# Spreading the decay rows with one bf16 product of three parts, and transposing v one step later

## The chip, the cores and the metric

The kernel runs on one core of a Trainium2 chip. The metric is the device time of one execution in microseconds (us); less is better. The engines of the core are TensorE (PE; its weight loads are listed as PEld), VectorE (DVE), ScalarE (ACT), GpSimd (POOL), SyncE (SP, which here only issues transfers) and the DMA engines.

## What is computed

Two layers of a decoder trunk over 256 tokens of width 1024. Layer 0 mixes by attention, layer 1 by a gated DeltaNet; after each mixer comes a mixture of experts (32 experts, top 2). All numbers are float32. The change lies in the DeltaNet, of which this much matters:

```python
h = x @ w_in                                    # qkv, z, b, a
qkv = silu(causal_dwconv(qkv, conv_w))          # 4 taps
q, k = l2norm(q), l2norm(k)                     # 8 heads of 128; v: 16 heads of 128
beta = sigmoid(b)
g = -exp(a_log) * softplus(a + dt_bias)
gc = cumsum(g)                                  # the decays, one row of numbers per head
decay = where(lower, exp(gc[:, None] - gc[None, :]), 0)
l_mat = where(strict, (k * beta) @ k.T * decay, 0)
# (I + l_mat) is inverted; u, w, the state and the output follow from it
o = o * rsqrt(mean(o * o) + eps) * norm_g * silu(z)
```

## The kernel before, in words

The order of work on every engine is written out by hand; engines meet only at counting semaphores.

**The projection steps.** The q, k and v channels are projected in 16 steps n = 0 to 15 of two 128-channel blocks each (q and k in steps 0 to 7, v in steps 8 to 15). In a step PE does `project(n, 0)` and `project(n, 1)` (L901, 8 products of 128 x 256 each), ACT copies the result out and scales it by one tap (`taps`), DVE adds the three other taps (`conv`, six instructions, L1700), ACT takes the tanh (L1265), and DVE makes the silu of it (L1690). Each engine runs through the same n in a loop of its own, so step n on DVE waits for step n on PE through ACT.

**The decay rows.** In steps 6 to 9 PE also calls `decay_rows` and `products` before each of the two projections, for the head pairs hk = 0 to 7. For each of the two heads of a pair, `decay_rows` needs the head's row of summed decays on all 128 partitions of a PSUM bank, 384 numbers wide (three blocks of 128). It gets it with a float32 product of a one-hot column, broadcast, and the 16 rows `g_row` (L928), and adds the causal mask with a bf16 product (L930). Then ACT takes the exponential of the bank (L1244 and L1245, four instructions a pair, semaphore `dt_sb`), and DVE multiplies it into the k k products (`decayed`, L1716). `decay_rows(hk)` waits for the exponentials of hk - 1, since both write banks 6 and 7. `g_row` is copied by ACT out of PSUM in step 3.

**The inversion.** From step 10 on DVE also inverts the 32 x 32 diagonal blocks: `blocks_in` (four transposes, L1730), then 31 calls of `eliminate` (L1738, L1740), five in each of the steps 11 to 15 and six behind them.

**The transposes of v.** `v_tokens(m)`, m = 8 to 15 (L957, four transposes on PE), waits for silu m (semaphore `si_sb`). It stands behind projection m + 2, the last two elsewhere. Its result is copied out by ACT (`evacuate_v`). vT has two buffers, so silu m on DVE, for m of 10 and more, waits until `v_tokens(m - 2)` is done (semaphore `vt_ps`).

**The z blocks.** Behind the steps PE does `z_block(0)` to `z_block(3)` (L971, eight products of 128 x 512), each followed by two `products(1, .)` (L944, L945). ACT takes a tanh of each block (`gate_z`, L1258); DVE then does, for each block, `z_gated` (L1722), two `decayed(1, .)` and one transpose of the inverse. Before the first `z_gated` it waits for all eight `v_tokens`:

```python
                dve.wait_ge(init, 8)
                dve.wait_ge(vt_ps, GH)
                for i in range(2):
                    z_gated(i)
                    for e in range(2):
                        decayed(1, 2 * i + e)
                    inverse_out(2 * i, 0)
```

`products(1, hk)` waits for `la_sb` of 8 + hk - 1, that is for `decayed(1, hk - 2)`, whose PSUM bank it writes again. Behind the z blocks come the levels of the inversion, the solves, the output projection and the experts of layer 1, each released by the work before it.

**The weights.** SP issues all loads of weights in one queue, each behind a count of PE's semaphores: the DeltaNet loads 3 to 10 behind `cv_ps` (projections done), the later ones behind `z_ps` (z blocks done). GpSimd sets one tile to zero (L583) behind `vt_ps` of 8.

Of the kernel before, what the change touches and what calls it, by code (L numbers as in the profile page):

```python
# [15 lines left out]
BF16 = mybir.dt.bfloat16  # L16
# [3 lines left out]
ALU = mybir.AluOpType  # L20
# [24 lines left out]
BLK = 32  # L45
INV = VH * NT
GROUPS = VH // 4
SOLVE_BANKS = (2, 3, 6, 7)
O_BANKS = ((4, 5), (6, 7), (0, 1), (2, 3))
EARLY = 5  # L50
# [139 lines left out]
def build(nc, a, out):  # L190
    with ExitStack() as ctx:
        def sb(name, shape, dt=F32):
            return ctx.enter_context(nc.sbuf_tensor(name, shape, dt))
# [18 lines left out]
        eps = sb("eps", [P, 1])  # L212
        mask_bf = sb("mask_bf", [P, P], BF16)
        ident_bf = sb("ident_bf", [P, 3, P], BF16)
        psum = [ctx.enter_context(nc.psum_tensor(f"bank{i}", [P, HALF], F32)) for i in range(8)]

        def k(name):
            at, w = COLS[name]
            return const[:, at:at + w]
# [71 lines left out]
        r = area(16, [VH, NT, GD])  # L291
        go = r
        ba_T = area(28, [SEQ])
        g_row = area(30, [3, P])
        xc = area(32, [2, 2, TAPS - 1 + SEQ])
        cv = area(36.0625, [2, 2, SEQ])
        ce = area(40.0625, [2, 2, SEQ])
# [294 lines left out]
        def _(pe):  # L592
# [266 lines left out]
            def gdn():  # L859
# [58 lines left out]
                def decay_rows(hk):  # L918

                    if hk == 0:  # L920
                        pe.wait_ge(gr_sb, 2)
                        pe.wait_ge(cw_sb, 1)
                    else:
                        pe.wait_ge(dt_sb, 4 * hk)
                    for e in range(2):
                        h = 2 * hk + e
                        bank = psum[6 + e][:, 0:384]
                        mm(bank, ident[0:VH, h:h + 1].to_broadcast([VH, P]),  # L928
                           g_row[0:VH].rearrange("p x c -> p (x c)"), start=True, stop=False)
                        last = mm(bank, mask_bf[:], ident_bf[:].rearrange("p x c -> p (x c)"), start=False, stop=True)  # L930
                    last.then_inc(row_ps, 1)

# [43 lines left out]
                for n in range(16):  # L976
                    for i in range(2):
                        if 6 <= n < 10:
                            decay_rows(2 * (n - 6) + i)
                            products(0, 2 * (n - 6) + i)  # L980
                        project(n, i)
                    if n == 0:
                        gate_tokens()
                    if n == 2:
                        decay_sums()
                    if 2 <= n < 10:
                        squares(n - 2)
                    if n >= 10:
                        v_tokens(n - 2)
                v_tokens(14)  # L990
                for i in range(4):
                    if i == 1:
                        v_tokens(15)
                    z_block(i)
                    for e in range(2):
                        products(1, 2 * i + e)

# [127 lines left out]
        def _(act):  # L1125
# [3 lines left out]
            def copy(o, i, **kw):  # L1129
                return do(o, i, ACT.Copy, **kw)  # L1130
# [86 lines left out]
            def gdn():  # L1217
# [37 lines left out]
                def gate_z(i):  # L1255

                    act.wait_ge(z_ps, i + 1)
                    do(zt[:, i], psum[i % 2][:], ACT.Tanh, scale=0.5).then_inc(zt_sb, 1)  # L1258

                for n in range(17):  # L1260
                    if n >= 1:
                        act.wait_ge(cv_sb, 2 * n)
                        if n >= 3:
                            act.wait_ge(si_sb, n - 2)
                        do(ce[:, (n - 1) % 2], cv[:, (n - 1) % 2], ACT.Tanh, scale=0.5).then_inc(ce_sb, 1)  # L1265
                    if n == 1:
                        act.wait_ge(min_sb, 1)
                        act.wait_ge(gdn_in, 80)
                        do(a_log, a_log, ACT.Exp).then_inc(sp_sb, 1)
                        own.link(do(ba_ln, ba_ln, ACT.Exp))  # L1270
                        do(ba_ln, ba_ln, ACT.Ln, bias=1.0).then_inc(sp_sb, 1)
                    if n == 6:
                        act.wait_ge(ss_ps, 4)
                        do(ln_k.rearrange("p t h -> p (t h)"), psum[2][:, 0:NT * GH], ACT.Ln, bias=eps[:]).then_inc(lnk_sb, 1)
                        act.wait_ge(lnk_sb, 1)
                        own.link(do(norm_k, ln_k, ACT.Exp, scale=0.5))
                        act.wait_ge(col_sb, 1)
                    if 6 <= n < 10:
                        for e in range(2):
                            decays(2 * (n - 6) + e)  # L1280
                    if n < 16:
                        taps(n)
                    if n == 3:
                        act.wait_ge(gr_ps, 1)
                        row = psum[4][0:VH, 0:SEQ].rearrange("p (x c) -> p x c", x=2)
                        copy(g_row[0:VH, 0:2], row).then_inc(gr_sb, 1)
                        copy(g_row[0:VH, 2], row[:, 1]).then_inc(gr_sb, 1)
                    if 1 <= n <= 8:
                        m = n - 1
                        act.wait_ge(si_sb, m + 1)  # L1290
                        if m >= 2:
                            act.wait_ge(ss_ps, m - 1)
                        do(sq[:, m % 2], gq[:, m // 4, 2 * (m % 4):2 * (m % 4) + 2], ACT.Square).then_inc(sq_sb, 1)
                    if n >= 10:
                        evacuate_v(n - 10)
                act.wait_ge(si_sb, 16)
                gate_z(0)
                evacuate_v(7)
                for i in range(1, 4):
                    gate_z(i)  # L1300

                def part(q, n=1):
                    return slice(q * BLK, (q + n) * BLK)
# [69 lines left out]
        def _(dve):  # L1373
# [71 lines left out]
            def attention():  # L1445
# [24 lines left out]
                for s in range(TURNS):  # L1470
                    n = head_at(s)
                    if n is not None:
                        b = n % 4
                        dve.wait_ge(s_ps, n + 1)
                        if n >= 4:
                            dve.wait_ge(pT_ps, n - 3)

                        v.scalar_tensor_tensor(out=s_sb[:, b], in0=psum[n % 2][:, 0:384], scalar=-ATT_SCALE,
                                               in1=k("mask_a" if n < 8 else "mask_b"), op0=ALU.mult,
                                               op1=ALU.subtract).then_inc(s_read, 1)  # L1480
                        dve.wait_ge(s_read, n + 1)
                        own(v.tensor_reduce(out=neg_max[:, b, 0:1], in_=s_sb[:, b, 0:P], axis=AX, op=ALU.min))
                        own.link(v.tensor_reduce(out=neg_max[:, b, 1:2], in_=s_sb[:, b, P:384], axis=AX, op=ALU.min))
                        dve.sem_inc(max_sb, 1)
                    m = head_at(s - 2)
                    if m is not None:
                        b = m % 4
                        dve.wait_ge(exp_sb, 2 * m + 2)
                        own.link(v.reciprocal(row_sum[:, b], row_sum[:, b]))
                        own(v.tensor_scalar(out=s_sb[:, b, 0:P], in0=s_sb[:, b, 0:P], scalar1=row_sum[:, b, 0:1],  # L1490
                                            scalar2=None, op0=ALU.mult))
                        own.link(v.tensor_scalar(out=s_sb[:, b, P:384], in0=s_sb[:, b, P:384], scalar1=row_sum[:, b, 1:2],
                                                 scalar2=None, op0=ALU.mult))
                        dve.sem_inc(p_sb, 1)
                    if s in (2, 4, 6, 8):
                        rotate(4 + (s - 2) // 2)
                    if s == 10:
                        own(v.tensor_copy(upper_b[:], k("upper")))
                        own(v.tensor_copy(ones_b[:], k("ones")))
                        own(v.tensor_copy(mask_bf[:], k("mask_a")[:, 0:P]))  # L1500
                        own(v.tensor_copy(ident_bf[:, 0], ident))
                        own(v.memset(ident_bf[:, 1], 0.0))
                        own(v.tensor_copy(ident_bf[:, 2], ident))
                layer_norm(0)

            def route(layer):
# [148 lines left out]
            def gdn():  # L1655
# [96 lines left out]
                for n in range(16):  # L1752
                    if n >= 1:
                        silu(n - 1)
                    if n == 1:
                        gate_logs()
                    if n == 4:
                        dve.wait_ge(gr_ps, 1)
                        v.tensor_tensor(out=col_bias, in0=ln_beta, in1=psum[5][:, 64:96].rearrange("p (t h) -> p t h", t=NT),
                                        op=ALU.subtract).then_inc(gc_sb, 1)  # L1760
# [115 lines left out]
```

## Time and profile before

| | |
|---|---|
| time of the runs, us | 1430.59, 1430.96, 1434.89 (median 1430.96) |
| profiled execution, us | 1432.51 |
| its span in the trace, us | 1430.6 |
| busy in the span | PE 1161.7 us, DVE 399.6 us, ACT 224.4 us |
| mean granted TensorE clock | 0.945 of full speed |
| DeltaNet projection steps and z blocks | 640 to 850 us of the span |

The span is the time from the first to the last instruction of the profiled execution; its time has 1.9 us more around it. Times in the rows below are counted from the start of the span. In rows of a timeline, an idle time in brackets is that of the engine just before the row, with what ended it.

### The profile page before, as it was taken

To read this page: it belongs to the slowest core of one execution; us is meant where nothing else is said; L and a number is where in the kernel's file an instruction comes from. 1 tells how busy PE (TensorE), PEld (TensorE's weight loads), DVE (VectorE), ACT (ScalarE), POOL (GpSimd) and SP (SyncE) were. 2 spreads that over 40 slices of the span, in tenths; PEclk is the share of its full clock that TensorE was granted. 3 is DMA by queue.
4 is the path that set the end of the run, shared out by engine and by line. 5 is a ranking of instruction groups with operands and counts; after the bars stand their busy time and mean duration, and the time that the engine had idled before them with its cause. 6 is when DMAs were issued, how large, how long until landed. Compare 5 with 4: busy or idle time off the path is not lost. (4 is left out here: it accounts for less than half of the span.)

```text
span 1430.6 us, 34064 instructions
## 1 busy us (share of the span) xinstructions
PE 1161.7 (81%) x14947; PEld 732.3 (51%) x14947; DVE 399.6 (28%) x1126; ACT 224.4 (16%) x589; POOL 14.4 (1%) x28
## 2 busy tenths in 40 slices
PE   8898779877777776759999899988987776777774
PEld 4444355544444444438778458445554444445442
DVE  1344512211111111133348744143211111111113
ACT  0123111100000010114433114110110010000001
POOL 0000100000000000010000000000000000000000
PEclk9999899989999999989999999998999999999998
DMA  9631599999999999973133341749999999999995
GB/s 361 253 118 59 211 412 425 429 423 429 424 427 427 426 427 424 427 302 118 59 118 118 118 146 62 281 198 379 424 429 425 425 426 426 427 426 428 425 424 209
DMA packets 63139, 461.20 MB, mean 322 GB/s; under 512 B 3824, under 2 KB 4000, under 8 KB 30320
## 3 DMA queue, kind: packets, MB, share of 16 engines
q1 hardware_dynamic: 61680, 455.92, 77.7%
q0 software_dynamic: 1408, 4.56, 0.8%
q8 instruction: 38, 0.62, 0.2%
q14 instruction: 13, 0.11, 0.0%
HBM read 459.41 MB, written 1.05 MB: 322 GB/s over the span
## 5 line engine op out<-in xcount | busy, mean ns | idle before, releaser
L803 PE MATMUL bank<-ring,arena 128*32 128x128 f32 x5568 | 191.4, 292 | 121.7 <-DMA ring<-in_moe_w 101.5
L803 PEld LDWEIGHTS bank<-ring,arena 128*32 128x32 f32 x5568 | 167.2, 114 | 142.7 <-DMA ring<-in_moe_w 82.5
L803 PE MATMUL bank<-arena 128*32 128x128 f32 x2624 | 103.2, 318 | 74.7 <-DMA arena<-in_moe_w 66.1
L1130 ACT ACTIVATE arena<-bank 128x256 f32<-128x256 f32 (+5 forms) x200 | 84.8, 431 | 368.6 <-PE bank L766 145.2
L1624 DVE SCALAR_TENSOR_TENSOR gated<-gated,bank 128x128 f32<-128x128 f32 x64 | 18.5, 288 | 428.4 <-ACT gated L1204 428.4
L763 PE MATMUL bank<-x,arena 128*32 128x256 f32 x1024 | 130.0, 637 | 4.5 <-DVEq L1585 4.5
L803 PEld LDWEIGHTS bank<-arena 128*32 128x32 f32 x2624 | 88.6, 125 | 85.8 <-DMA arena<-in_moe_w 79.3
L901 PE MATMUL bank<-xT,ring 128*128 128x256 f32 x512 | 115.2, 382 | 0.0
L901 PEld LDWEIGHTS bank<-xT,ring 128*128 128x128 f32 x512 | 96.6, 192 | 13.0 <-issue 0.4
L1204 ACT ACTIVATE gated<-bank 128x128 f32<-128x128 f32 x64 | 17.8, 278 | 466.7 <-PE bank L803 466.7
L784 PE MATMUL bank<-arena 32*128 32x256 f32 x1056 | 86.5, 444 | 4.8 <-issue 3.6
L639 PE MATMUL bank<-ring,xT 128*128 128x512 f32 x192 | 87.0, 606 | 2.3 <-DVEq L1466 2.0
L817 PE MATMUL bank<-ring,hT 128*32 128x256 f32 x1408 | 85.1, 382 | 3.3 <-DMA ring<-in_moe_w 3.3
L1630 DVE COPY arena<-bank 128x256 f32<-128x256 f32 x62 | 26.3, 425 | 185.0 <-PE bank L766 185.0
L784 PEld LDWEIGHTS bank<-arena 32*128 32x128 f32 x1056 | 54.2, 211 | 26.6 <-issue 21.4
L639 PEld LDWEIGHTS bank<-ring,xT 128*128 128x128 f32 x192 | 36.2, 194 | 44.6 <-issue 43.9
L971 PE MATMUL bank<-ring,xT 128*128 128x512 f32 x128 | 58.8, 613 | 0.0
L817 PEld LDWEIGHTS bank<-ring,hT 128*32 128x32 f32 x1408 | 41.6, 109 | 33.0 <-issue 10.7
L1100 PE MATMUL bank<-ring,arena 128*128 128x512 f32 x128 | 55.9, 594 | 1.6 <-ACT arena L1130 1.6
L763 PEld LDWEIGHTS bank<-x,arena 128*32 128x32 f32 x1024 | 29.4, 119 | 51.0 <-issue 38.9
L1633 DVE COPY arena<-bank 128x256 f32<-128x256 f32 x64 | 27.2, 425 | 99.1 <-PE bank L817 99.1
L1700 DVE SCALAR_TENSOR_TENSOR arena<-arena,cw 128x256 f32<-128x256 f32 x96 | 42.3, 482 | 40.2 <-ACT arena L1130 38.8
(229 smaller groups left out, 990.6 us busy)
## 6 DMA issues: line engine op xcount, KB each, us to landing
ring<-in_moe_w SPq DMA_DIRECT2D x131, 2048.0 KB, 40.5
arena<-in_moe_w SPq DMA_DIRECT2D x61, 2048.0 KB, 40.0
ring<-in_gdn_w_in SPq DMA_DIRECT2D x12, 2048.0 KB, 8.8
ring<-in_ab_w_in SPq DMA_DIRECT2D x5, 2048.0 KB, 23.1
ring<-in_gdn_w_out SPq DMA_DIRECT2D x4, 2048.0 KB, 8.6
ring<-in_ab_w_out SPq DMA_DIRECT2D x2, 2048.0 KB, 19.6
ring<-in_ab_w_in SPq DMA_DIRECT2D x2, 1024.0 KB, 8.2
x<-in_x SPq DMA_DIRECT2D x2, 512.0 KB, 4.4
```

The source lines that it names most:

```text
L639: last = mm(psum[4 + t][:], xT[:, j, t * P:(t + 1) * P], ring[:, slot_att(n), j], start=(j == 0), stop=(j == DJ - 1))
L763: mm(psum[4][h * CAP:(h + 1) * CAP, 0:Q].rearrange("p (c q) -> p c q", c=2), pick[:, b, t], by_j[:, h::TILES], start=(t == 0), stop=(t == ...
L784: last = mm(psum[h][:, t * Q:(t + 1) * Q], gpT[part, b, t], y_e[part], start=False, stop=stop and t == NT - 1, skip_group_check=not (stop ...
L803: last = mm(psum[5][h * CAP:(h + 1) * CAP, m * FH:(m + 1) * FH], xeT[:, j], slot_tile(slots[m])[:, j, h // 2 * SEQ + h % 2:(h // 2 + 1) * ...
L817: last = mm(psum[7][h * CAP:(h + 1) * CAP, 0:Q], hT[:, g], w2[:, g // 2, g % 2, h * Q:(h + 1) * Q], start=(g == 0), stop=(g == TILES - 1), ...
L901: last = mm(psum[n % 2][:, i * SEQ:(i + 1) * SEQ], ring[:, slot_gdn(n // 2), j, ch * P:(ch + 1) * P], xT[:, j], start=(j == 0), stop=(j == ...
L971: last = mm(psum[i % 2][:], xT[:, j, t * P:(t + 1) * P], ring[:, slot_gdn(8 + zz), j], start=(j == 0), stop=(j == DJ - 1))
L1100: last = mm(psum[GDN_OUT + 2 * h + t][:], goT[:, 8 * g + c, t * P:(t + 1) * P], ring[:, slot_gdn(12 + 2 * g + h), c], start=(g == 0 and c ...
L1130: return do(o, i, ACT.Copy, **kw)
L1630: o2.link(v.tensor_copy(gpT[:, (b + 1) % GROUP].rearrange("p t q -> p (t q)"), psum[5][:, 0:SEQ]))
L1633: o2.link(v.tensor_copy(y_e, psum[7][:, 0:Q]))
L1700: ins = v.scalar_tensor_tensor(out=cv[:, b, i], in0=xc[:, b, i, tap:tap + SEQ], scalar=cw[:, at:at + 1], in1=cv[:, b, i], op0=ALU.mult, op ...
```

## The change

Two edits.

1. The fp32 product of `decay_rows` becomes a bf16 one. The decay rows are split into three bf16 parts whose sum is the float32 value: the value rounded to bf16, the rest rounded to bf16, and the rest of that. They stand at partitions 0, 32 and 64 of `g_row`, which becomes a bf16 tile of 80 rows with zeros between, and the one-hot column `head_bf` (bf16) picks the head's row of all three parts, so that one product adds them. DVE sets the tile to zero in step 2 and makes the parts in step 3 (five instructions); ACT, which made two copies in step 3, makes one in step 4. `head_bf` is made by DVE in the attention of layer 0.
2. `v_tokens(m)` stands behind projection m + 3 in place of m + 2: those of 8 to 12 behind projections 11 to 15, that of 13 ahead of `z_block(0)`, that of 14 behind `z_block(0)`, that of 15 behind `z_block(1)`. Before, that of 14 stood ahead of `z_block(0)` and that of 15 ahead of `z_block(1)`. `evacuate_v` on ACT moves with them.

```diff
+G_ROWS = 2 * 32 + VH
...
+        head_bf = sb("head_bf", [P, VH], BF16)
...
-        g_row = area(30, [3, P])
+        g_rest = area(29, [SEQ])
+        g_mid = area(30, [SEQ], BF16, 2)
+        g_row = area(30.5, [3, P], BF16, 2)
...
                     if hk == 0:
-                        pe.wait_ge(gr_sb, 2)
+                        pe.wait_ge(gr_sb, 4)
...
-                        mm(bank, ident[0:VH, h:h + 1].to_broadcast([VH, P]),
-                           g_row[0:VH].rearrange("p x c -> p (x c)"), start=True, stop=False)
+                        mm(bank, head_bf[0:G_ROWS, h:h + 1].to_broadcast([G_ROWS, P]),
+                           g_row[0:G_ROWS].rearrange("p x c -> p (x c)"), start=True, stop=False)
...
-                    if n >= 10:
-                        v_tokens(n - 2)
-                v_tokens(14)
+                    if n >= 11:
+                        v_tokens(n - 3)
                 for i in range(4):
-                    if i == 1:
-                        v_tokens(15)
+                    if i == 0:
+                        v_tokens(13)
                     z_block(i)
+                    if i < 2:
+                        v_tokens(14 + i)
                     for e in range(2):
                         products(1, 2 * i + e)
...
-                    if n == 3:
-                        act.wait_ge(gr_ps, 1)
-                        row = psum[4][0:VH, 0:SEQ].rearrange("p (x c) -> p x c", x=2)
-                        copy(g_row[0:VH, 0:2], row).then_inc(gr_sb, 1)
-                        copy(g_row[0:VH, 2], row[:, 1]).then_inc(gr_sb, 1)
+                    if n == 4:
+                        act.wait_ge(gr_sb, 3)
+                        copy(g_row[0:G_ROWS, 2], g_row[0:G_ROWS, 1]).then_inc(gr_sb, 1)
...
-                    if n >= 10:
-                        evacuate_v(n - 10)
+                    if n >= 11:
+                        evacuate_v(n - 11)
                 act.wait_ge(si_sb, 16)
-                gate_z(0)
-                evacuate_v(7)
-                for i in range(1, 4):
+                for i in range(4):
                     gate_z(i)
+                    if i < 2:
+                        evacuate_v(6 + i)
...
+                        own(v.tensor_copy(head_bf[:], k("stack")[:, 0:VH]))
...
+                    if n == 2:
+                        own(v.memset(g_row[0:G_ROWS].rearrange("p x c -> p (x c)"), 0.0))
+                    if n == 3:
+                        dve.wait_ge(gr_ps, 1)
+                        own.wait()
+                        row = psum[4][0:VH, 0:SEQ]
+                        first, mid = (g_row[at:at + VH, 0:2].rearrange("p x c -> p (x c)") for at in (0, 32))
+                        last = g_row[64:64 + VH, 0:2].rearrange("p x c -> p (x c)")
+                        v.tensor_copy(first, row).then_inc(gr_sb, 1)
+                        dve.wait_ge(gr_sb, 1)
+                        own.link(v.tensor_tensor(out=g_rest[0:VH], in0=row, in1=first, op=ALU.subtract))
+                        own.link(v.tensor_copy(g_mid[0:VH], g_rest[0:VH]))
+                        v.tensor_copy(mid, g_mid[0:VH]).then_inc(gr_sb, 1)
+                        v.tensor_tensor(out=last, in0=g_rest[0:VH], in1=g_mid[0:VH], op=ALU.subtract).then_inc(gr_sb, 1)
```

## Rows read from the trace of the kernel before

**Rows 1.** Groups of the page, most costly first: expert products of layers 0 and 1.
```profile
L803 PE MATMUL bank<-ring,arena 128*32 128x128 f32 x5568 | 191.4, 292 | 121.7 <-DMA ring<-in_moe_w 101.5
```

**Rows 2.** Busy time of the engines, steps 10 to 15: stretch, its length, then each engine.
```profile
745.00:803.00 58.00, 53.14 (x241) 43.23 (x241) 50.57 (x114) 17.67 (x41) 0.12 (x1) 0.97 0.41 141
```

**Rows 3.** Timeline of PE, steps 6 to 8 (start us, us, engine, line, operation).
```profile
695.70 0.91 PE L928 MATMUL bank<-arena,const 16*128 16x384 f32 x2 [0.55 <-ACT ring L1245]
...
701.93 0.95 PE L914 MATMUL bank<-const,arena 128*128 128x1 f32 x8
702.81 0.91 PE L928 MATMUL bank<-arena,const 16*128 16x384 f32 x2
703.65 0.34 PE L930 MATMUL bank<-ident_bf,mask_bf 128*128 128x384 bf16 x1
703.91 0.91 PE L928 MATMUL bank<-arena,const 16*128 16x384 f32 x2
704.75 0.34 PE L930 MATMUL bank<-ident_bf,mask_bf 128*128 128x384 bf16 x1
704.92 0.59 PE L944 MATMUL bank<-arena 128*128 128x256 f32 x2
...
709.13 0.91 PE L928 MATMUL bank<-arena,const 16*128 16x384 f32 x2
...
715.35 0.95 PE L914 MATMUL bank<-const,arena 128*128 128x1 f32 x8
```

**Rows 4.** Timeline of ACT, step 7.
```profile
702.13 0.60 ACT L1130 ACTIVATE arena<-bank 128x512 f32<-128x512 f32 x1 [2.75 <-PE bank L901]
...
706.24 0.63 ACT L1265 ACTIVATE arena<-arena 128x512 f32<-128x512 f32 x1 [2.27 <-DVE arena L1700]
...
707.74 0.37 ACT L1245 ACTIVATE ring<-bank,gates 128x128 f32<-128x128 f32 x1
```

**Rows 5.** Timeline of DVE: steps 3, 10 and 12, then the first z block.
```profile
672.17 2.71 DVE L1700 SCALAR_TENSOR_TENSOR arena<-arena,cw 128x256 f32<-128x256 f32 x6 [5.15 <-ACT arena L1130]
...
747.94 7.88 DVE L1730 STREAM_TRANSPOSE y<-ring 32x1024 f32<-32x1024 f32 x4
...
766.27 0.69 DVE L1690 SCALAR_TENSOR_TENSOR arena<-arena 128x512 f32<-128x512 f32 x1 [0.76 <-issue]
...
802.63 0.19 DVE L1740 TENSOR_TENSOR y<-y,arena 128x31 f32<-128x31 f32 x1
803.03 0.69 DVE L1722 SCALAR_TENSOR_TENSOR arena<-arena,bank 128x512 f32<-128x512 f32 x1 [0.20 <-DVE y L1740]
803.63 1.81 DVE L1716 TENSOR_TENSOR ring<-bank,ring 128x768 f32<-128x768 f32 x2
```

**Rows 6.** Timeline of PE: behind projection 12, then from projection 15 to `z_block(2)`.
```profile
764.69 0.60 PE L957 MATMUL bank<-const,arena 128*128 128x128 f32 x4
...
786.73 0.60 PE L957 MATMUL bank<-const,arena 128*128 128x128 f32 x4
792.18 1.12 PE L957 MATMUL bank<-const,arena 128*128 128x128 f32 x4 [4.86 <-DVE arena L1690]
793.09 7.98 PE L971 MATMUL bank<-ring,xT 128*128 128x512 f32 x16
800.91 0.59 PE L944 MATMUL bank<-arena 128*128 128x256 f32 x2
...
802.22 0.60 PE L957 MATMUL bank<-const,arena 128*128 128x128 f32 x4
802.65 7.03 PE L971 MATMUL bank<-ring,xT 128*128 128x512 f32 x16
...
810.83 7.03 PE L971 MATMUL bank<-ring,xT 128*128 128x512 f32 x16
```

**Rows 7.** Stretches of 1 us; behind the engines, the granted clock (1.00 is full speed).
```profile
690.00:691.00 1.00, 1.00 (x5) 0.84 (x4) 0.48 (x2) 0.48 (x1) 0.00 (x0) 0.50 1.01 365
...
793.00:794.00 1.00, 1.00 (x4) 0.48 (x3) 0.93 (x3) 0.29 (x1) 0.00 (x0) 0.50 1.06 414
```

## Prediction

> **What bounds the kernel now.** I began with the groups of the page. Most of the time is in the experts, where PE waits for weights to arrive [rows 1]; the change does not touch that, but it decides what a gain in layer 1's mixer is worth. Every load there is issued behind a semaphore count of PE or DVE, none at a fixed time, so if the DeltaNet ends x us sooner, the experts of layer 1 start and end x us sooner. The question is by how much PE reaches the work behind the z blocks sooner.
>
> The timelines give the stretch around the change. In steps 6 to 9 PE runs without a gap: a step takes 715.35 - 701.93 = 13.42 us [rows 3], and DVE and ACT wait for it. From step 10 on the bound changes. DVE takes in the blocks for 7.88 us at 747.94 and then has no gap over 0.8 us until its last elimination ends at 802.82 [rows 5]; in 745 to 803 it is busy 50.57 of 58 us, the rest being mostly the short spaces between dependent instructions [rows 2]. PE is ahead of it, until `v_tokens(14)` has to wait 4.86 us for DVE's silu [rows 6]. So the stretch has two limits in a row: PE sets when DVE starts its long chain (step 9), and DVE sets when it ends. What shortens PE before step 10 moves DVE's whole chain; what shortens PE after that only helps as far as DVE lets it.
>
> **Edit 1, the rows.** For a head, L928 takes 703.65 - 702.81 = 0.84 us and L930 0.26 (703.65 to 703.91) or, for the second head, 0.17 (704.75 to 704.92): 2.11 us for a pair [rows 3]. The new product streams the same 384 columns in bf16, once, as L930 does. Its cost on the stream is not in the trace for 80 rows; the nearest rows bound it: 0.17 where the weight load is hidden, 0.26 where it isn't. Four such products make 0.68 to 1.04 us a pair. I take 0.80, nearer to the hidden end, because the 80 rows are nearer to the 128 of the products before which the load was hidden (L944) than to the 16 before which it wasn't (L928). A pair saves 1.31 us (1.07 to 1.43).
>
> By the Trainium skill (TensorE: Matmul & The Clock Gate, Back-to-back issue gap) a warm product of 384 columns takes 384/2.4 + 2.5 ns, about 0.16 us, so an estimate from that page for the pair is 0.65 us and the saving 1.46; the row of 0.17 agrees where the load is hidden, and the rule leaves out the 0.26.
>
> Does each saving reach the end of the step? The second `decay_rows` of a step waits for the exponentials of the first pair. Their chain starts where projection 1 of the step before ended: PE goes on to L914 at 701.93, ACT copies from 702.13, DVE convolves, the tanh starts at 706.24, and the last of the four exponentials ends at 707.74 + 0.37 = 708.11 [rows 4]. With a few hundredths for the semaphore the second L928 could start 6.22 us after 701.93. PE itself will be there after 0.88 (L914, 701.93 to 702.81) + 0.80 + 4.21 (products and projection 0: 704.92 to 709.13) [rows 3] = 5.89. So ACT's chain, hidden by 1 us before, is now last by 0.33 us, and a step takes 6.22 + 0.80 + 4.11 (715.35 - 709.13 = 6.22, less the pair's 2.11) = 11.13 us, 2.29 less than 13.42. That holds for steps 7, 8 and 9. In step 6 the wait is there already, 0.55 us for L1245 at 695.70 [rows 3], so the saving of its first pair only lengthens the wait (to 1.9 us), and that of the second, 1.31, is left. Sum: 1.31 + 3 x 2.29 = 8.2 us. With 1.04 a pair it is 1.07 + 3 x 2.05 = 7.2, with 0.68 it is 1.43 + 3 x 2.41 = 8.7.
>
> What it adds: in step 2 a memset and in step 3 five short instructions on DVE. The copies of 16 rows or of a few dozen numbers are some 0.2 to 0.3 us each, with their waits under 2 us together; DVE idles 5.15 us in step 3 [rows 5], and the first user is step 6. Without that cover it would cost its 2 us. ACT swaps two short copies in step 3 for one in step 4, ahead of a square: under 0.3 us, where its gaps are 2.75 and 2.27 us in a later step [rows 4]. `head_bf` is one DVE copy in the attention, at most 0.2 us, if on the path at all. I put all three at 0 (0 to 0.3).
>
> **Edit 2, the transposes.** All times here are those of before, from which the 8.2 is then taken off. Projection 15 with its transposes ended at 786.73 + 0.43 = 787.16 (0.43 is 802.65 - 802.22) [rows 6]. Now `v_tokens(13)` ends there, and its silu has long been done. `z_block(0)` starts at 787.16 and not at 793.09. The block itself took 7.82 us in place of 6.87 (810.83 - 802.65 = 8.18, less the products' 1.31): the clock was at half after the wait [rows 7]. So: `z_block(0)` to 794.03, `v_tokens(14)` to 794.46 (its silu ended near 792.1), two products to 795.77, `z_block(1)` to 802.64, `v_tokens(15)` to 803.07, two products. Without a new wait `z_block(2)` would start at 804.38, 6.45 us sooner than 810.83.
>
> But there is a new wait. `products(1, 2)` needs `decayed(1, 0)`, and DVE reaches it only after the last elimination (802.82), after all eight `v_tokens` (now the last of them ends at about 803.24, a little later than the eliminations) and after `z_gated(0)`. That gives `z_gated` at 803.4 (before: 803.03), `decayed(1, 0)` from 804.0 to 804.9 and `decayed(1, 1)` to 805.8, from the 0.60 and 0.90 of [rows 5]. `products(1, 2)` starts at 804.95, `products(1, 3)` at 805.85, `z_block(2)` at 806.5: 2.1 us of new waiting, and 4.3 us gained. Queued behind the waiting product on PE are the z blocks and everything after them, so these 2.1 us count in full. From there PE leads again: DVE's turn for a block (0.6 + 1.8 + 2.2) is shorter than PE's 8.18, so the 4.3 us stay.
>
> Three queues that the edit moves past. Silu m waits for `v_tokens(m - 2)`, now one step later. The tightest I find is silu 11 at 766.27 [rows 5]: it will need the transposes that now stand where those at 764.69 stand [rows 6], 0.43 earlier, so ending near 764.9: 1.4 us of slack. Cost 0; without the slack it would land on the saturated DVE at full price. ACT's copies of v have their turns one step later behind the same taps; their results are wanted by transposes two heads on. SP's counts are of projections and z blocks; each load is issued sooner by what its releaser gains, so its distance to its use stays, and nothing is lost there. GpSimd's memset behind `vt_ps` is wanted only a level later.
>
> **Sum.** 8.2 + 4.3 = 12.5 us. The profiled execution would take 1432.51 - 12.5 = 1420.0; it is 1.55 above the median of the runs, so against the median 1430.96 I predict 1418.5.
>
> **The rivals.**
> (a) *The clock falls in one of the new waits.* At 690 to 691 the clock was at half (1.2 GHz) while PE was busy throughout, behind a run of small products and decay rows [rows 7], and part of that was hidden before the wait of 0.55 us. Now step 6 has a wait of 1.9 us, or about 3.5 if the clock does not fall in front of it, and `products(1, 2)` one of 2.1. The wait of 4.86 was followed by a stretch at half whose price was 0.48 on the transposes (793.09 - 792.18, less 0.43) and 0.95 on the z block, 1.4 us. One such fall in the open: 1418.5 + 1.4 = 1419.9; two: 1421.3. Against it: the wait of 0.55 cost nothing, and both new waits are well under 4.86. Chance of one or two 0.30. The Trainium skill (TensorE: Matmul & The Clock Gate, HAM oscillation) warns of idle gaps between bursts of products, after which the clock is at its lower level; the trace agrees for the wait of 4.86, and by that rule one fall more is 1.4 us more.
> (b) *The loop through ACT and DVE eats more of edit 1.* It is already the last by 0.33 us; each further us in a step costs one in each of three steps. At 1 us more the time is 1421.5; if edit 1 gives nothing and only edit 2 works, 1426.7. For it: the chain has no slack left. Against: its pieces were timed in a trace where only its start waited for PE, and DVE's `decayed` of the pair does not stand in it. Chance 0.14.
> (c) *Given back later*, by weights that don't come sooner: 1430. No load in the stretch is released by time, and no load ended a wait of PE in the timeline rows that I read there. Chance 0.05.
> (d) *Slower.* Silu m waits for the later transposes. The slack is 1.4 us; DVE is the bound in steps 11 to 15, so each us of lateness beyond it is lost once per step, six times. To outweigh 12.5 us PE must be late by 1.4 + 12.5/6 = 3.5 us against DVE in every step; at 5 us late the time is 1418.5 + 6 x 3.6 = 1440.1. It takes a clock at half through these steps, whose projections would double from 7 us. Chance 0.03.
> (e) *More than forecast*, below 1416.4: the new products or ACT's chain shorter than in the rows: 0.06.
>
> **How the numbers follow.** The forecast has what is left, 0.42, with 7.2 to 8.7 for edit 1 and 4.3 for edit 2: 1418.0 to 1419.5, and a us of scatter on each side (two of the runs differ by 0.4, one is 4 higher). For 8 in 10 I add (a) and the near half of (b): 1416.4 to 1423.0. A measurement of this kernel can tell about 0.3%, 4.3 us, from no change. Faster by more than that (below 1426.7) are the forecast, (a), (e) and nearly all of (b): 0.91; within it (c) and the rest of (b): 0.06; slower 0.03.
>
> **What would show it.** (Lines as of the kernel before.) L928 as 16 products of 80 rows with starts 0.17 to 0.26 us before the next; steps 7 to 9 at 11.1 us (from 13.42) with a wait of 0.3 for L1245 and step 6 with a wait for L1245 of 1.9 us or more; DVE's L1730 at about 739.7; no wait of L957 for L1690; a wait of L944 for DVE's L1716 of about 1.9 us and then one of 0.3 behind `z_block(1)`; `z_block(2)` at 798.3. The prediction is wrong if L930 is followed by gaps, if L1690 on DVE waits for L957, or if the clock column shows 0.50 somewhere between 696 and 830.

## The result and the profile after

| | before | after |
|---|---|---|
| median of the runs, us | 1435.49 (1430.59 to 1439.01, 6 runs) | 1422.49 (1419.77 to 1424.08, 6 runs) |
| profiled execution, us | 1432.51 | 1424.08 |
| its span, us | 1430.6 | 1422.2 |

The ratio of the runs is 0.9923, with a 95% interval of 0.9903 to 0.9942: 11 us faster (8 to 14). Forecast were 1418.5 in a range of 1416.4 to 1423.0, a ratio of 0.9913. The runs of before that came with the result were slower than the three shown ahead of it, so the ratio is the better measure of the two. For the profiled execution the forecast was 1420.0 us; it took 1424.08, 4.1 us more.

The timeline of PE after the change, with start, length, line and the idle time ahead; L932 is the new bf16 product, L934 the mask, L905 the projections, L918 the squares, L961 `v_tokens`, L948 `products`, L975 the z blocks. It answers to [rows 3] and [rows 6]:

```profile
689.12 0.95 PE L918 MATMUL bank<-const,arena 128*128 128x1 f32 x8
689.93 0.32 PE L932 MATMUL bank<-arena,head_bf 80*128 80x384 bf16 x1
690.10 0.33 PE L934 MATMUL bank<-ident_bf,mask_bf 128*128 128x384 bf16 x1
690.26 0.33 PE L932 MATMUL bank<-arena,head_bf 80*128 80x384 bf16 x1
690.42 0.33 PE L934 MATMUL bank<-ident_bf,mask_bf 128*128 128x384 bf16 x1
690.59 0.59 PE L948 MATMUL bank<-arena 128*128 128x256 f32 x2
...
698.62 0.34 PE L932 MATMUL bank<-arena,head_bf 80*128 80x384 bf16 x1 [3.76 <-ACT ring L1250]
...
700.77 4.46 PE L905 MATMUL bank<-xT,ring 128*128 128x256 f32 x16
705.07 0.95 PE L918 MATMUL bank<-const,arena 128*128 128x1 f32 x8
...
711.30 0.34 PE L932 MATMUL bank<-arena,head_bf 80*128 80x384 bf16 x1 [0.50 <-ACT ring L1250]
...
716.08 0.95 PE L918 MATMUL bank<-const,arena 128*128 128x1 f32 x8
...
738.10 0.95 PE L918 MATMUL bank<-const,arena 128*128 128x1 f32 x8
...
782.19 1.04 PE L961 MATMUL bank<-const,arena 128*128 128x128 f32 x8
783.07 7.03 PE L975 MATMUL bank<-ring,xT 128*128 128x512 f32 x16
...
798.55 0.60 PE L961 MATMUL bank<-const,arena 128*128 128x128 f32 x4
800.97 0.70 PE L948 MATMUL bank<-arena 128*128 128x256 f32 x2 [1.82 <-DVE ring L1720]
...
802.59 7.03 PE L975 MATMUL bank<-ring,xT 128*128 128x512 f32 x16
```

The reader is to see five things. A pair of decay rows takes 690.59 - 689.93 = 0.66 us. The steps 7, 8 and 9 take 716.08 - 705.07 = 11.01 us, with a wait of 0.50 for ACT in each. Step 6, from 689.12 to 705.07, takes 15.95 us, with a wait of 3.76. `v_tokens(12)` and `(13)` run together at 782.19 with no wait, and so does `v_tokens(14)`, which now stands behind `z_block(0)`: the wait of 4.86 us is gone. And PE has a new wait of 1.82 us, for DVE's `decayed(1, 0)`.

The granted clock of a stretch behind the wait of 3.76 us is the number behind the engines: 0.51, so the lower of the two levels (1.2 GHz), and the projection that starts in it takes 4.46 us in place of 3.62:

```profile
699.00:702.00 3.00, 3.00 (x10) 2.46 (x9) 1.43 (x2) 1.35 (x4) 0.00 (x0) 0.51 0.00 0
```

DVE and ACT, for [rows 4] and [rows 5]: the first and the last of the five new DVE instructions of step 3 with the `conv` behind them, the tanh and the last exponential of the first pair of step 7 on ACT, then DVE's long chain:

```profile
669.85 0.41 DVE L1769 CAST arena<-bank 16x256 bf16<-16x256 f32 x1
...
671.30 0.42 DVE L1774 TENSOR_TENSOR arena<-arena 16x256 bf16<-16x256 f32 x1
675.08 2.71 DVE L1704 SCALAR_TENSOR_TENSOR arena<-arena,cw 128x256 f32<-128x256 f32 x6 [3.37 <-ACT arena L1135]
```

```profile
709.38 0.63 ACT L1270 ACTIVATE arena<-arena 128x512 f32<-128x512 f32 x1 [2.27 <-DVE arena L1704]
...
710.87 0.38 ACT L1250 ACTIVATE ring<-bank,gates 128x128 f32<-128x128 f32 x1
```

```profile
743.84 7.85 DVE L1734 STREAM_TRANSPOSE y<-ring 32x1024 f32<-32x1024 f32 x4
...
762.14 0.69 DVE L1694 SCALAR_TENSOR_TENSOR arena<-arena 128x512 f32<-128x512 f32 x1 [0.76 <-issue]
...
798.88 0.19 DVE L1744 TENSOR_TENSOR y<-y,arena 128x31 f32<-128x31 f32 x1
```

DVE still idles 3.37 us behind its new instructions. The chain from the block transposes to the last elimination is as long as before, 799.07 - 743.84 = 55.2 us against 802.82 - 747.94 = 54.9, and silu 11 still has 0.76 us ahead of it and no wait for PE: the whole chain moved and kept its length to 0.3 us. (The 0.3 us stand ahead of silu 14, 1.12 us of idle time in place of 0.76. Edit 1 alone, where `v_tokens` stands as before, has them too, and edit 2 alone has not, so they are no wait for the later transposes.)

To compare kernels I use a stretch that leaves out what happens elsewhere: from the squares of step 5 (the first row above) to `z_block(2)`. Rows of PE of the kernel before that are not among those shown, the two groups ahead of the steps among them:

```profile
639.01 1.07 PE L869 MATMUL bank<-xT,wba 128*32 128x256 f32 x16 [0.87 <-DVE xT L1379]
640.01 7.17 PE L901 MATMUL bank<-xT,ring 128*128 128x256 f32 x32
...
686.21 0.95 PE L914 MATMUL bank<-const,arena 128*128 128x1 f32 x8
...
742.20 0.95 PE L914 MATMUL bank<-const,arena 128*128 128x1 f32 x8
```

and the same two of the kernel after:

```profile
639.61 1.93 PE L873 MATMUL bank<-xT,wba 128*32 128x256 f32 x16 [0.88 <-DVE xT L1382]
641.47 8.62 PE L905 MATMUL bank<-xT,ring 128*128 128x256 f32 x32
```

Before, the stretch takes 810.83 - 686.21 = 124.62 us; after, 802.59 - 689.12 = 113.47, so 11.15 less. From `z_block(2)` to the end of the span it is 619.8 before and 619.6 after: all that is won there stays. Ahead of the squares the profiled execution of after is 2.91 us later (0.60 at the gate columns, the rest in these two groups, which ran at the lower clock: 1.93 against 1.07 us and 8.62 against 7.17). In the kernel with edit 2 alone, where nothing of the change has run by then, the two groups took 1.94 and 7.92 us, and in the other experiments 1.93 or 1.94 and 7.85 to 8.38. So the one profile of before is the exception in having the gate columns at the higher clock, and nothing of the change is needed for the lower one. The three add up to the 8.4 us between the two profiled executions, and explain why these differ by less than the medians do.

### The profile page after: what moved, and what is told of

It is laid out like the page before. It is cut to its first block and busy times, and to the rows that moved or that the text cites. A ratio compares the mean times of both kernels' runs of the same rounds, so it can differ in the third digit from the quotient of the medians.

```text
span 1422.2 us, 34039 instructions
## 1 busy us (share of the span) xinstructions
PE 1149.7 (81%) x14931; PEld 726.4 (51%) x14931; DVE 401.2 (28%) x1133; ACT 223.8 (16%) x588; POOL 14.4 (1%) x28
## 5 line engine op out<-in xcount | busy, mean ns | idle before, releaser
L807 PE MATMUL bank<-ring,arena 128*32 128x128 f32 x5568 | 181.3, 282 | 119.5 <-DMA ring<-in_moe_w 97.1
L807 PEld LDWEIGHTS bank<-ring,arena 128*32 128x32 f32 x5568 | 159.4, 110 | 139.2 <-DMA ring<-in_moe_w 82.5
L807 PE MATMUL bank<-arena 128*32 128x128 f32 x2624 | 108.1, 329 | 81.5 <-DMA arena<-in_moe_w 77.4
L1135 ACT ACTIVATE arena<-bank 128x256 f32<-128x256 f32 (+4 forms) x198 | 84.1, 431 | 373.9 <-PE bank L770 147.1
L807 PEld LDWEIGHTS bank<-arena 128*32 128x32 f32 x2624 | 92.8, 129 | 92.4 <-DMA arena<-in_moe_w 86.7
L905 PE MATMUL bank<-xT,ring 128*128 128x256 f32 x512 | 116.3, 385 | 0.0
L905 PEld LDWEIGHTS bank<-xT,ring 128*128 128x128 f32 x512 | 97.6, 194 | 13.8 <-issue 0.8
L821 PE MATMUL bank<-ring,hT 128*32 128x256 f32 x1408 | 88.2, 392 | 3.3 <-DMA ring<-in_moe_w 3.3
L975 PE MATMUL bank<-ring,xT 128*128 128x512 f32 x128 | 58.4, 610 | 0.0
```

What stands on the lines that cost most here:

```text
L807: last = mm(psum[5][h * CAP:(h + 1) * CAP, m * FH:(m + 1) * FH], xeT[:, j], slot_tile(slots[m])[:, j, h // 2 * SEQ + h % 2:(h // 2 + 1) * ...
L821: last = mm(psum[7][h * CAP:(h + 1) * CAP, 0:Q], hT[:, g], w2[:, g // 2, g % 2, h * Q:(h + 1) * Q], start=(g == 0), stop=(g == TILES - 1), ...
L905: last = mm(psum[n % 2][:, i * SEQ:(i + 1) * SEQ], ring[:, slot_gdn(n // 2), j, ch * P:(ch + 1) * P], xT[:, j], start=(j == 0), stop=(j == ...
L975: last = mm(psum[i % 2][:], xT[:, j, t * P:(t + 1) * P], ring[:, slot_gdn(8 + zz), j], start=(j == 0), stop=(j == DJ - 1))
```

## The experiments

In each, "the stretch" is the one just defined; before 124.62, changed kernel 113.47. The line numbers shift by a few from kernel to kernel. Each kernel has one profile, and a ratio is always that of its timed runs to those of the kernel before.

**Edit 1 alone.** The v parts as in the kernel before:

```diff
-                    if n >= 11:
-                        v_tokens(n - 3)
+                    if n >= 10:
+                        v_tokens(n - 2)
+                v_tokens(14)
...
```

> Edit 1 alone; v_tokens and evacuate_v stand as before. My theory (PE sets when DVE's long chain starts, DVE sets when it ends): DVE's L1730 starts sooner by edit 1's whole saving, 7.0 us as in the changed kernel if the clock falls behind the wait of step 6 (8.6 if not), the wait of v_tokens(14) for silu 14 stays at 4.9 us and z_block(2) comes 7.0 us sooner than before, counted from the squares of step 5: 117.6 us between them (before 124.62, changed kernel 113.47). Time about 7 us under the kernel before. Rival (the two edits only work together, since PE waited 4.9 us for DVE anyway): the wait grows by 7 us and the time moves by under 2.

Measured: ratio to before 0.9954 (0.9939 to 0.9968). PE:

```profile
733.83 0.95 PE L918 MATMUL bank<-const,arena 128*128 128x1 f32 x8
784.15 1.11 PE L961 MATMUL bank<-const,arena 128*128 128x128 f32 x4 [5.19 <-DVE arena L1693]
785.06 9.39 PE L975 MATMUL bank<-ring,xT 128*128 128x512 f32 x16
```

The stretch, from 685.02 to 804.22, is 119.2 us: 5.4 less than before, 1.6 less than expected. From the squares of step 5 to those of step 9 it won 7.2 us (7.0 expected). The wait for silu 14 stayed (5.19 us, not 7 more), and the clock was at its lower level behind it for longer than in the kernel before: `z_block(0)` took 9.39 us and not 7.98, which is where the 1.6 went. So edit 1 moves DVE's chain, as forecast, and the rival falls.

**Edit 2 alone**, the fp32 product of before with the v parts of after.

> Edit 2 alone, with the fp32 product of before. My theory: from the squares of step 5 to z_block(2) 120.3 us (4.3 less than before), with a new wait of products(1, 2) for DVE's first decayed(1, 0) of about 1.9 us; time 4 us under before. Rival 1 (the wait only moves): under 1 us gained, the new wait about 5 us. Rival 2 (the whole wait and its stretch at half clock are won): 118.2 us, 6.4 less.

Measured: ratio 0.9957 (0.9936 to 0.9978).

```profile
687.43 0.95 PE L914 MATMUL bank<-const,arena 128*128 128x1 f32 x8
...
696.93 0.91 PE L928 MATMUL bank<-arena,const 16*128 16x384 f32 x2 [2.23 <-ACT ring L1246]
...
746.75 0.95 PE L914 MATMUL bank<-const,arena 128*128 128x1 f32 x8
...
809.62 0.70 PE L944 MATMUL bank<-arena 128*128 128x256 f32 x2 [1.82 <-DVE ring L1717]
811.25 7.03 PE L971 MATMUL bank<-ring,xT 128*128 128x512 f32 x16
```

From step 9's squares to `z_block(2)` it is 811.25 - 746.75 = 64.5 us against 810.83 - 742.20 = 68.6 before: 4.1 us won, with the same new wait of 1.82. The first part of the stretch, which the edit does not touch, was 3.3 us longer in this profile (59.3 against 56.0), with the clock at its lower level at 707 to 710 and at 735 to 737 while PE was busy; so the whole stretch was 123.8 us, 0.8 under before and not the expected 4.3. These falls are not in the profile of before, whose fall at 689 is not in this one: they come and go. And without that fall the wait of step 6 is 2.23 us and not 0.55, while the step takes 15.73 us against 15.72. The two edits alone won 6.6 and 6.2 us in the timed runs, together 11.0: within their intervals (4.6 to 8.7, 3.2 to 9.2, 8.3 to 13.9) they add, and so do the parts of the stretch that each moves, 7.2 + 4.1 = 11.3 against 11.15.

**One more step later.** Does lateness of the transposes cost as I said in rival (d)?

```diff
-                    if n >= 11:
-                        v_tokens(n - 3)
+                    if n >= 12:
+                        v_tokens(n - 4)
                 for i in range(4):
                     if i == 0:
+                        v_tokens(12)
                         v_tokens(13)
...
```

ACT's copies of v move one step back too, the sixth of them behind silu 15.

> The changed kernel with v_tokens one more step later: 8 to 11 behind projections 12 to 15, 12 and 13 ahead of z_block(0), 14 and 15 as in the changed kernel. Silu 10 then waits for transposes behind projection 12, some 5 us later than it ran. My forecast's rival (d) says that lateness on the saturated DVE is lost once per step, six times: up to 30 us slower than the changed kernel, 1450 us. The other theory: the first wait pushes DVE's chain back by some 5 us, and after that DVE, whose steps of 8 us are longer than PE's 7.34, no longer waits: about 5 us slower than the changed kernel, once.

Measured: 1.0016 of before (0.9999 to 1.0033), so all that the change won is lost, some 13 us; the stretch is 129.1 us, 15.6 more than the changed kernel's. First DVE, then PE:

```profile
758.89 0.69 DVE L1696 SCALAR_TENSOR_TENSOR arena<-arena 128x512 f32<-128x512 f32 x1 [6.00 <-PE bank L961]
...
766.23 0.69 DVE L1696 SCALAR_TENSOR_TENSOR arena<-arena 128x512 f32<-128x512 f32 x1 [1.17 <-PE bank L961]
...
774.75 0.69 DVE L1696 SCALAR_TENSOR_TENSOR arena<-arena 128x512 f32<-128x512 f32 x1 [1.29 <-PE bank L961]
```

```profile
785.30 0.69 PE L961 MATMUL bank<-const,arena 128*128 128x128 f32 x4 [2.30 <-ACT arena L1136]
793.91 1.09 PE L961 MATMUL bank<-const,arena 128*128 128x128 f32 x4 [7.91 <-ACT arena L1136]
794.79 9.32 PE L975 MATMUL bank<-ring,xT 128*128 128x512 f32 x16
```

On DVE the other theory was right: beyond the 0.76 us that silu always waits, it lost 5.2 us once and 0.4 and 0.5 after it, not 6 us six times. But both theories missed where the rest went. `v_tokens(12)` and `(13)` write banks that ACT has to have copied out two heads earlier, and ACT makes those copies behind the tanh that waits for DVE. So PE stood 10.2 us in front of `z_block(0)`, with work ready behind it in its queue, and the clock fell. Rival (d)'s price per step was wrong, and its bound of where the change would turn slower too: one step further is enough to lose everything, by another queue.

**Few rows or an fp32 neighbour?** Only the first bf16 part is kept (`G_ROWS = VH`), so the decays are rounded to bf16 here, and DVE makes one instruction of the five in step 3.

> The changed kernel with the first bf16 part of the decay rows alone, so a product of 16 rows and not of 80 (the decays are then only as exact as bf16). I sized the product at 0.80 us a pair because I took the 0.26 us behind L930 for a price of a weight load of few rows; measured were 0.66 with 80 rows. If few rows are the cause, a pair takes 0.8 to 1.0 here; if it was the fp32 product behind it, 0.66 again.

Measured, one run:

```profile
704.00 0.33 PE L932 MATMUL bank<-arena,head_bf 16*128 16x384 bf16 x1
704.27 0.34 PE L934 MATMUL bank<-ident_bf,mask_bf 128*128 128x384 bf16 x1
704.53 0.33 PE L932 MATMUL bank<-arena,head_bf 16*128 16x384 bf16 x1
704.80 0.34 PE L934 MATMUL bank<-ident_bf,mask_bf 128*128 128x384 bf16 x1
704.97 0.59 PE L948 MATMUL bank<-arena 128*128 128x256 f32 x2
```

Each start is 0.27 us behind the last, and a pair takes 704.97 - 704.00 = 0.97, though all is bf16. With 80 rows a start is 0.16 to 0.17 behind the last. So it is the few rows: next to a product of 128 rows, one of 16 costs 0.1 us more on either side of it, one of 80 nothing. The rows of the weight loads show the 0.1 us: with 80 rows the load for the mask's product starts at 705.88 and the product at 706.04, so it is hidden behind the product before; with 16 rows they start at 704.26 and 704.27, so it is not. The forecast's upper bound, 0.26 for each product, was real, for another shape.

**The wait of step 6, filled.** Eight more fp32 products where PE waits; the output does not use them.

```diff
                         project(n, i)
+                        if n == 6 and i == 0:
+                            for j in range(8):
+                                mm(psum[3][:, SEQ:2 * SEQ], xT[:, j, 0:P], xT[:, j], start=True, stop=True)
```

> The changed kernel with eight more fp32 products of 128 x 256 (3.5 us, into an unused half bank) behind projection (6, 0), where PE waits 3.76 us for the exponentials of the first pair; the output is unchanged. Theory A: the clock's fall behind that wait is the wait's doing; with the wait filled it is gone, step 6 takes 14.3 us and not 15.95, and from the squares of step 5 to z_block(2) are 111.8 us and not 113.47. Theory B: it has to do with the decay rows and squares around it, as in the kernel before, where it came with PE busy: step 6 stays at 15.9.

```profile
685.51 0.95 PE L918 MATMUL bank<-const,arena 128*128 128x1 f32 x8
...
695.01 0.34 PE L932 MATMUL bank<-arena,head_bf 80*128 80x384 bf16 x1 [0.31 <-ACT ring L1253]
...
699.78 0.95 PE L918 MATMUL bank<-const,arena 128*128 128x1 f32 x8
```

Step 6 takes 14.27 us, no row of steps 6 to 9 is at the lower clock, and the stretch is 112.0: theory A. The ratio to before was 0.9866 (0.9838 to 0.9894, four runs), some 8 us under the changed kernel's, where the stretch accounts for 1.5. The profiled execution is 5.0 us under that of the changed kernel, and 3.6 of these are won ahead of the squares of step 5, where both do the same work; so the rest is not shown to be the filled wait's doing. With four runs, two at 1419 and two at 1411 us, I leave it open.

**The logarithm earlier.** What sets the wait is the work of ACT ahead of the first exponentials.

```diff
-                    if n == 6:
-                        act.wait_ge(ss_ps, 4)
-                        do(ln_k.rearrange("p t h -> p (t h)"), psum[2][:, 0:NT * GH], ACT.Ln, bias=eps[:]).then_inc(lnk_sb, 1)
-                        act.wait_ge(lnk_sb, 1)
-                        own.link(do(norm_k, ln_k, ACT.Exp, scale=0.5))
                         act.wait_ge(col_sb, 1)
...
                         do(sq[:, m % 2], gq[:, m // 4, 2 * (m % 4):2 * (m % 4) + 2], ACT.Square).then_inc(sq_sb, 1)
+                    if n == 5:
+                        act.wait_ge(ss_ps, 4)
+                        do(ln_k.rearrange("p t h -> p (t h)"), psum[2][:, 0:NT * GH], ACT.Ln, bias=eps[:]).then_inc(lnk_sb, 1)
+                        act.wait_ge(lnk_sb, 1)
+                        own.link(do(norm_k, ln_k, ACT.Exp, scale=0.5))
```

and DVE's subtraction of it stands ahead of silu 5.

> The changed kernel with ACT's logarithm and exponential of the norms (and their two table loads, 3.1 us) one step earlier, in ACT's gap behind the square of step 5, and DVE's short instruction that needs them ahead of silu 5. If that work of ACT sets the wait of 3.76 us, the wait is about 1.2, step 6 is 2.6 us shorter, and 1.7 more if the clock then does not fall: 109.2 us from the squares of step 5 to z_block(2), against 113.47. Rival: tanh 5 now comes 0.9 us later, DVE's silu too, and under 1 us is won.

Measured: 0.9889 (0.9869 to 0.9908); the stretch, 688.05 to 797.46, is 109.4 us, step 6 11.89.

```profile
695.17 0.34 PE L932 MATMUL bank<-arena,head_bf 80*128 80x384 bf16 x1 [1.38 <-ACT ring L1250]
...
699.94 0.95 PE L918 MATMUL bank<-const,arena 128*128 128x1 f32 x8
```

The 4.1 us are there, as expected, and the clock stays up behind a wait of 1.38.

**DVE's order behind silu 15.**

```diff
                 silu(15)
+                for e in range(2):
+                    decayed(1, e)
                 for k_ in range(5 * EARLY + 2, BLK - 1):
                     eliminate(k_)
...
                     z_gated(i)
-                    for e in range(2):
-                        decayed(1, 2 * i + e)
+                    if i:
+                        for e in range(2):
+                            decayed(1, 2 * i + e)
```

> The changed kernel with decayed(1, 0) and (1, 1) on DVE right behind silu 15, ahead of the last four eliminations. If the order on DVE, not its sum of work, makes products(1, 2) wait, that wait (1.82 and 0.33 us) is gone, and z_block(2), which needs z_gated(0), comes 2.0 us sooner: 111.4 us from the squares of step 5. Rival: z_gated(0) comes later by the 1.8 us of the two decayed, and z_block(2) waits for it: nothing won.

Measured: 0.9904 (0.9886 to 0.9922); the stretch is 112.4 us.

```profile
797.50 7.10 PE L975 MATMUL bank<-ring,xT 128*128 128x512 f32 x16 [1.19 <-DVE arena L1726]
```

Between the two: the wait of `products(1, 2)` is gone, and a part of it is back as a wait of 1.19 us of `z_block(2)` for `z_gated(0)`, which now comes later. 1.1 us won of the 2.0.

**All three together**: the earlier logarithm (e6), DVE's order (e7), and the exponentials of the first pair ahead of the tanh in steps 7 to 9:

```diff
+                    if 7 <= n < 10:
+                        decays(2 * (n - 6))
                     if n >= 1:
                         act.wait_ge(cv_sb, 2 * n)
...
                     if 6 <= n < 10:
-                        for e in range(2):
+                        for e in range(n > 6, 2):
                             decays(2 * (n - 6) + e)
```

> e6 and e7 together, and in steps 7 to 9 the exponentials of the first pair ahead of the tanh on ACT, where ACT idles 2.26 us and they take 1.34; that takes away the 0.50 us for which PE waits in each of these steps. 4.3 + 2.0 + 1.5: 105.7 us from the squares of step 5 to z_block(2), and about 8 us less than the changed kernel, ratio to before 0.987. Rival: the tanh is late and DVE's chain with it, and the three steps stay at 11.0 us: 107.2.

```profile
700.80 0.95 PE L918 MATMUL bank<-const,arena 128*128 128x1 f32 x8
...
711.15 0.95 PE L918 MATMUL bank<-const,arena 128*128 128x1 f32 x8
...
795.03 7.11 PE L975 MATMUL bank<-ring,xT 128*128 128x512 f32 x16 [0.84 <-DVE arena L1729]
```

Steps 7 to 9 take 10.35 us each, without a wait, and the stretch is 795.03 - 688.91 = 106.1 us. Median 1413.85 us, ratio to before 0.9860 (0.9840 to 0.9880, four runs): faster than both kernels.

## Which step of the prediction failed, and what was right

**The step that failed is step 6.** The forecast let the saving of its first pair go into the wait ("to 1.9 us") and kept that of the second, 1.31 us. The wait became 3.76, the clock fell behind it, and the step took 15.95 us against 15.72 (701.93 - 686.21) before: 0.2 lost in place of 1.31 won. The forecast had read the wait of 0.55 as the step's own, though in that profile PE reached it late, at the lower clock of 689 to 692.6; edit 2 alone, with the same rows as before and no such fall, has a wait of 2.23 in a step just as long. The new wait cost nothing by itself either: the exponentials let PE go on 9.50 us behind the squares (698.62 - 689.12), as before (9.49). What cost was the clock, 1.7 us, now in the open. The filled wait shows it, since with PE kept busy step 6 is 14.27 us, near the forecast's 15.72 - 1.31 = 14.41, and so does the earlier logarithm. Why the clock fell at 689 in the kernel before was not tried.

This is rival (a), at its "about 3.5", to which the forecast gave 0.30; and of its three signs of being wrong the last one came, 0.50 in the clock column at 700 to 702. That the median still lies among the forecast's times is the width of its range, which took (a) in.

**What bounds the stretch.** Right. DVE's chain moved whole with the end of PE's step 9 and kept its length (55.2 and 54.9 us); edit 1 alone left the wait for silu 14 in place, edit 2 alone took it away and brought the new one.

**A pair of rows.** Forecast 0.80, measured 0.66, just under the lower bound of 0.68. The choice between the bounds was the wrong one: with 80 rows beside 128 nothing is added. The rule of the Trainium skill (TensorE: Matmul & The Clock Gate, Back-to-back issue gap) gave an estimate of 0.65, and for these shapes the trace agrees; for 16 rows it does not (0.97, against the same 0.65).

**Steps 7 to 9.** Forecast 11.13 us with a wait for L1245 of 0.33, measured 11.01 with 0.50 (L1250 is the same line). That ACT's chain would be the last was right, and it is why a step won 2.41 us and not 2 x 1.45 = 2.9, which the cheaper pairs alone would have given.

**Edit 1 in sum.** 8.2 forecast, 7.0 measured (55.99 to 48.98 us from step 5's squares to step 9's): 0.4 us more in the three steps, 1.5 less in step 6.

**Edit 2.** 4.3 forecast, 4.1 measured (68.63 to 64.49); the new waits 1.9 and 0.3 forecast, 1.82 measured, with no second wait in the rows; but the two products behind it took 802.59 - 800.97 = 1.62 us, where they took 1.31 before. The three queues cost nothing: silu waited for no transposes, no load ended a wait, and the new DVE work in step 3 sat in an idle time that is still 3.37 us long.

**Sum.** 12.5 forecast, 11.15 in the stretch, 11 in the runs; but 8.4 between the two profiled executions, for the 2.91 us ahead of the stretch. Rivals (b), (c) and (e) did not come. Rival (d) had the right mechanism to fear and a wrong price, as its experiment shows. That 1422.49 is 4.0 us above the forecast's 1418.5 is not all missed saving: the runs of before that stand beside it had a higher median too, 1435.49 and not 1430.96.

## What to carry to other kernels

When PE and DVE take turns at being the bound, find the instruction at which the lead changes hands: a saving ahead of it moves the whole chain behind it, a saving behind it is worth only what the other engine's last dependency lets through. A saving ahead of an existing wait makes that wait longer, and a longer wait can have a price of its own, the clock; so look at what is late in that wait first (here an ACT logarithm and its table loads, worth 4 us for moving its three instructions). And where a step is postponed, read the slack of each queue that it releases, the copies that free its buffers too: here one step was free and two cost 13 us.

## What the runs showed of the hardware

- bf16 products of 384 columns follow each other in 0.165 us when their rows are 80 and 128 in turn, and in 0.27 when they are 16 and 128 in turn: then the weight load of 0.1 us is not hidden behind the product before.
- The clock stood at half (1.2 GHz) behind the wait of step 6 in all five profiles in which that wait was 3.37 to 3.76 us (the changed kernel and four of the experiments), and in none of the five in which it was 0.31 to 2.23 (the kernel before and edit 2 alone among them). It cost 1.7 us in the changed kernel, 1.5 in edit 1 alone, and in the one-part kernel, where it lasted from 695 to 701.7, 3.1 us (step 6 took 17.71 us, without it 14.6 by its slower rows). The wait of 1.82 ahead of the products in front of `z_block(2)` was followed by it in two of the six profiles that have it (8.57 and 8.59 us for the block in place of 7.03).
- It also falls while PE is busy throughout: at 689 before, behind squares and fp32 decay rows, and at 707 and 735 with edit 2 alone. No such fall was seen between steps 6 and 9 in the kernels with the bf16 rows other than behind the wait of step 6.
